# Loading weight chunks in pairs: one 2 MB transfer and one semaphore for every two ring buffers

## The reference

```
x = x + sum over the token's two experts e of  gate_e * ((silu(x @ w_gate[e]) * (x @ w_up[e])) @ w_down[e])
```

## Time and profile before

| | us |
|---|---|
| median of 3 runs | 2662.08 |
| lowest and highest | 2660.66, 2671.79 |
| the profiled execution, its own time | 2671.94 |
| its span in the trace | 2670.3 |

### The profile page before, as it was taken

One profiled execution on the slowest core, in us unless ns is written; L12 is line 12 of the kernel. 1 busy time (PEld: TensorE's weight loads), 2 busy tenths in 40 slices (PEclk: granted clock), 3 DMA queues, 4 the chain that ended last, 5 costly groups with the idle time before them and its releaser, 6 DMA issues.

```text
span 2670.3 us, 37525 instructions
## 1 busy us (share of the span) xinstructions
PE 2516.6 (94%) x13426; PEld 2120.9 (79%) x13426; DVE 1840.2 (69%) x2063; ACT 1442.2 (54%) x1434; POOL 56.3 (2%) x71
## 2 busy tenths in 40 slices
PE   8979999998899999999999998999999999999995
PEld 7758799896688998868998867878787877778784
DVE  4535687745466876735445646888888888888886
ACT  4454444344544444523443523777777777777773
POOL 0010000000100000000000001000000000000000
PEclk9989999999899999959999968999999999999997
DMA  6305545432154555507653413999999999999996
GB/s 257 142 4 203 204 158 188 174 143 95 64 198 174 180 188 177 177 21 221 220 189 128 156 61 142 389 357 372 361 369 357 367 361 363 364 356 369 358 368 251
DMA packets 93278, 615.78 MB, mean 231 GB/s; under 512 B 9712, under 2 KB 17536, under 8 KB 21632
## 3 DMA queue, kind: packets, MB, share of 16 engines
q1 hardware_dynamic: 88544, 591.51, 60.1%
q0 software_dynamic: 4640, 23.03, 2.3%
HBM read 599.30 MB, written 15.20 MB: 230 GB/s over the span
## 4 chain that ended last, share of the span: by engine, by line
PE 54%; issue 32%; DVE 5%; ACT 4%; DVEq 2%; POOL 1%; ACTq 1%; DMA 0%; POOLq 0%
PE bank L306 16%; PE bank L308 15%; PE bank L307 15%; DVE w_lo L594 2%; ACT w_hi L474 2%; PE bank L392 2%; DVEq L586 2%; PE bank L417 1%; PE bank L1373 1%; PE bank L402 1%; DVE probs L657 0%; DVE x_tok L1782 0%; ACT arena L1554 0%; PE bank L1256 0%; PE bank L1253 0%
## 5 line engine op out<-in xcount | busy, mean ns | idle before, releaser
L594 DVE TENSOR_TENSOR w_lo<-raw,w_hi 128x2048 fp32r<-128x2048 f32 x550 | 1248.3, 2290 | 424.5 <-ACT w_hi L474 384.1
L474 ACT CAST w_hi<-raw 128x2048 fp32r<-128x2048 f32 x550 | 1050.5, 1913 | 484.3 <-PE bank L308 471.6
L306 PE MATMUL bank<-w_hi,hT_hi 128*128 128x512 f32 (+3 forms) x1360 | 538.2, 396 | 20.5 <-DVE w_lo L594 14.0
L308 PE MATMUL bank<-w_hi,hT_lo 128*128 128x512 f32 (+3 forms) x1360 | 525.9, 387 | 0.0
L307 PE MATMUL bank<-w_lo,hT_hi 128*128 128x512 f32 (+3 forms) x1360 | 525.8, 387 | 0.0
L306 PE MATMUL bank<-hT_hi,w_hi 128*128 128x256 f32 (+1 forms) x1568 | 450.7, 287 | 6.2 <-DVEq L612 5.9
L307 PE MATMUL bank<-hT_lo,w_hi 128*128 128x256 f32 (+1 forms) x1568 | 445.0, 284 | 0.0
L308 PE MATMUL bank<-hT_hi,w_lo 128*128 128x256 f32 (+1 forms) x1568 | 445.0, 284 | 0.0
L306 PE MATMUL bank<-w_hi,oT_hi 128*128 128x512 f32 x876 | 344.1, 393 | 17.8 <-DVE oT_lo L1957 11.1
L307 PE MATMUL bank<-w_lo,oT_hi 128*128 128x512 f32 x876 | 342.4, 391 | 0.0
L308 PE MATMUL bank<-w_hi,oT_lo 128*128 128x512 f32 x876 | 342.3, 391 | 0.0
(11 more groups left out here) (266 smaller groups left out, 1814.4 us busy)
## 6 DMA issues: line engine op xcount, KB each, us to landing
raw<-in_weights_dram SPq DMA_DIRECT2D x554, 1024.0 KB, 6.9
token_rows<-all_cols SPq DMA_DIRECT2D x11, 512.0 KB, 7.5
arena<-in_norms_dram POOLq DMA_DIRECT2D x2, 2048.0 KB, 8.3
nat<-token_rows POOLq DMA_DIRECT2D x8, 512.0 KB, 8.0
unit_rows<-probs POOLq DMA_DIRECT2D x8, 512.0 KB, 8.8
arena<-in_b_gate_dram POOLq DMA_DIRECT2D x2, 1536.0 KB, 7.0
unit_rows<-all_cols SPq DMA_DIRECT2D x4, 512.0 KB, 9.8
tables<-in_tables_b_dram POOLq DMA_DIRECT2D x1, 1216.0 KB, 6.0
```

The lines of the kernel that those rows point to most:

```text
L306: mm(out, st[0], mv[0], start=start, stop=False, skip_group_check=True)
L308: return mm(out, st[1], mv[0], start=False, stop=stop, skip_group_check=True)
L474: self.isa.copy(m.w_hi[:, slot, :], m.raw[:, raw, :]).then_inc(m.hi_ready, 1)
L594: self.isa.tensor_tensor(m.w_lo[:, slot, :], m.raw[:, raw, :], m.w_hi[:, slot, :].bitcast(F32), ALU.subtract).then_inc(m.lo_ready, 1)
```

## The change

The ring keeps its six buffers, now taken as three neighbouring pairs. A load brings two chunks in one DMA of 2 MB, whose source has the two chunks' 8 KB side by side for each partition (16 KB in a row); the host lays the weights out so. There is one `raw_full` semaphore for a pair. SP's load of chunks c and c+1 waits for what the load of c+1 alone waited for (VectorE done with c-5), and ScalarE's copy of either chunk waits for the whole pair. The writes of zeros to DRAM now stand one behind each pair. The counts (212, 42, 6) are all even, so no pair spans two lists. Nothing else changes.

```diff
-        self.raw_full = [sem(f"raw_full{i}") for i in range(RAW)]
+        self.raw_full = [sem(f"raw_full{i}") for i in range(RAW // 2)]
...
-            self.eng.wait_ge(m.raw_full[raw], loads * 16)
+            self.eng.wait_ge(m.raw_full[raw // 2], loads * 16)
...
-            def load(chunk):
-                raw, _, _, number = w.take()
+            def load_two(pair):
+                raw, _, _, _ = w.take()
+                _, _, _, number = w.take()
                 sp.wait_ge(m.lo_ready, number + 1)
-                sp.dma_start(m.raw[:, raw, :], inp["weights"][chunk]).then_inc(m.raw_full[raw], 16)
-
+                sp.dma_start(m.raw[:, raw:raw + 2, :], inp["weights"][pair]).then_inc(m.raw_full[raw // 2], 16)
...
             with w.repeat(before, {"chunks": RAW}) as i:
-                for j in range(RAW):
-                    load(i * RAW + j)
+                for j in range(RAW // 2):
+                    load_two(i * (RAW // 2) + j)
             sp.wait_ge(m.blank, w.next(m.blank))
-            for c in range(before * RAW, FIXED + RAW):
-                load(c)
+            for c in range(before * RAW // 2, (FIXED + RAW) // 2):
+                load_two(c)
                 if blanks:
                     blank(*blanks.pop(0))
...
-                    for j in range(first, end):
-                        load(expert * UNIT + (FIXED + j))
+                    for j in range(first // 2, end // 2):
+                        load_two(expert * (UNIT // 2) + (FIXED // 2 + j))
...
-        "weights": np.stack(chunks),
+        "weights": np.stack(chunks).reshape(-1, 2, P, CH).transpose(0, 2, 1, 3),
```

## The result

The changed kernel takes 2671.44 us (median of 20 runs, 2665.79 to 2675.01), the kernel before 2660.34 us (median of 20, 2659.3 to 2671.79) in the same comparison. The ratio is 1.0032, 95% interval 1.0024 to 1.0041: about 8.5 us slower. (The two medians are 11.1 us apart, the two means 8.7 us, since some executions of the kernel before are slow too.) The forecast was +2.5 us and "the same"; the direction holds and the bound of 0.5% too, but the size is three to four times the forecast's, and it sits elsewhere. One thing must be known to read the times: the executions of the kernel before fall into two main groups by TensorE's granted clock, most at 2658 to 2664 us (mean clock 0.955 to 0.959), a smaller one at 2671 to 2672 us (0.952), with few between them, and the profile shown ahead of the prediction was of the second group.

The account below looks back on a forecast made before the run. The prediction took TensorE to set the pace, with loads landing before they are wanted. Start 1.5, expert stage 0, its head 0.5 and the end 0.5 summed to +2.5 us on 2662.08, giving 2664.6 us, range 2655 to 2684.

Parts of the forecast that it names:

- What bounds it: Expert stage: TensorE sets the pace, loads land before they are wanted, and the DMA engines' 97% is not yet a bound.
- The pair's landing: Expert stage: a 2 MB pair lands 7.3 to 9.8 us after its issue, taken as 8.3.
- The 10.4 us that a pair may take: Chunks 288 and 289: 9.4 us until ScalarE's copy plus 1.0 us of VectorE's other work before TensorE is late.
- Expert stage: From 1750 to 2600 us: pairs land in time, 0 us, with 0 to +8 for the spread of landings.
- The start: First pair lands when chunk 1 did, so ScalarE's first copies and TensorE's first product come later: +1.5 us.
- The head of the expert stage: Loads beside the scatters land later, 8.4 us plus 1 to 2.5 for a pair: 0 to 2 us, taken as +0.5.
- The end: The last pair may run beside GpSimd's last result write: 0 to +1.7 us, taken as +0.5.
- Ahead of the experts: Closest pair found has 13.9 us until its first copy and needs 7.3, so nothing moves: 0 us.
- The base: Profiled execution of 2671.94 us, 9.9 above the three runs' median; the forecast was put on that median, 2662.08.
- The range: Whole kernel: terms give 2663 to 2675 us, widened to 2655 to 2684 for run spread and rival 2's near end.
- rival 2: Expert stage: mean landing over about 10.5 us makes ScalarE wait for loads; slower, such as 2684 or 2724 us; chance 0.10.
- Rival 1: Expert stage: the DMA engines' 97% really paces the loads, so fewer transfers give time back, 2648 us; chance 0.05.

Follow-up runs that it names:

- r8_before_third: The kernel before with no edit, run again for a third profile; 2660.89 us.
- r10_before_warm26: The kernel before with 26 instead of 30 idle products in the second model's warm-up (`turn_x`, four times); 2667.28 us, ratio 1.0014.
- r9_changed_warm34: The changed kernel with 34 instead of 30 idle products in the second model's warm-up (`turn_x`, four times); 2663.79 us, ratio 1.0008.

## Why the prediction was right, and where it was wrong

- **What bounds it** (TensorE, with the ring ahead of it): right. Half as many transfers gave no time, and the waits for `w_lo` are unchanged.
- **The pair's landing**, taken as 8.3 us: too low. Its median was 9.3 in the first profile, 8.3 to 9.1 in six others with pairs there, inside the bounds of 7.3 and 9.8; the maximum is 11.2. From 400 to 800 us, where a single load lands in 4.8 us, the pair's median was 7.7, so the second MB cost 2.9 us there and not the 2.5 of the lower bound.
- **The 10.4 us that a pair may take**: borne out by the followed pair, which landed in 10.0 and cost nothing. "No row has the copy waiting for a weight DMA" was wrong, though, and by the prediction's own numbers: it gave ScalarE's copy 9.4 us, so a landing between 9.4 and 10.4 had to show as a wait of ScalarE that VectorE's other work hides. The profile has 43 such waits, 58.2 us.
- **Expert stage, 0 with 0 to +8**: right. Seven units: +1.6 us in one profile, 0 to +0.5 in the others.
- **The start, +1.5**: +1.4 measured at TensorE's first product. By VectorE's end with chunk 71, executions of one and the same kernel lie up to 2 us apart, but on the mean the four profiles with a pair at the start are 1.7 us behind the ten others, so the term stays.
- **The head of the expert stage, +0.5**: in the first profile the copies waited 16.5 us for loads from 1640 to 1750 us, and VectorE's end with chunk 262, counted from its end with chunk 220, came 2.9 us later than in r8_before_third; in the second profile nothing was lost. The 2.9 is above the term's own bound of 2.
- **The end, +0.5**: nothing.
- **Ahead of the experts, "Nothing moves"**: this is the step that failed. No engine there waits for a load, as I wrote. But the sum took the granted clock as given. The pairs' later moment alone (r5_asked_late) moves the time to 2669.0 us, single loads ahead of the experts (r4_experts_pairs) bring it to 2664.2, and in the profile of the changed kernel the clock from 1110 to 1240 us is 0.76 where it was 0.83, with 6.3 us lost there and 2.9 us more from 1465 to 1590.
- **The base**: the profiled execution was 9.9 us above the median of its own three runs, and I carried the difference along as noise. It was this same clock pattern, and asking which stretch held it would have shown that 10 us hang on where the clock falls.
- **The range**, 2655 to 2684: that 2671.4 lies in it is in part luck. It was that wide for late landings in the expert stage, for rival 2 and for the spread of the three runs; none of its terms was the clock's.
- **Rival 2** had the right sign for the wrong reason; its condition, a mean landing over 10.5 us, did not come. Rival 1 fell.

Open: how the changed moments lead, through 600 us of equal work, to the longer fall at 1130 us. The fall near 537 us is the first difference seen, but r10_before_warm26 loses time without it and r9_changed_warm34 regains it with it. Why TensorE stands at the branch in one case and not in the other is open too.

## What to carry to other kernels

Before trusting a sum of waits to a few microseconds, see how the kernel's executions spread and what the granted clock does in each stretch of a slow and a quick one; here, where the clock falls in thinly filled stages, a shift of a microsecond ahead of them cost or gave more than the edit itself. A transfer that landed after its reader was ready cost nothing here while the next engine in the chain was at other work; follow one case to the engine that sets the pace. Grouping loads made the ring coarser and gave nothing, since nobody waited for the engines' time; look for such a wait before trying it.

## What the runs showed of the hardware

- A 2 MB load of 16 KB rows from 1750 to 2600 us lands in 7.4 to 7.6 us at the least and 8.3 to 9.3 in the median, beside a stream of its like; a load of 1 MB in 4.7 to 5.5 and 6.7 to 7.3. From 400 to 800 us, where the loads come further apart, the medians are 7.7 and 4.8.
- For the same 363 GB/s the DMA share is 0.95 with pairs and 0.96 to 0.98 with single loads asked for one by one, but 0.92 with single loads asked for two at a time.
- The same kernel without an edit took 2659.2 and 2671.9 us, with the same work done and the clock from 1110 to 1240 us at 0.83 and 0.76.
- Four idle products of 0.23 us each, added or taken away at four places, moved the median by 7.7 us down, 3.4 us up and 5.4 us up; only for the first do the intervals stand clearly apart.
- TensorE's time at the lower clock was between 222 and 259 us in 14 profiles, least in the shortest span, 2656.5 us, and most in the longest, 2672.6 us.
